# Two-layer decoder trunk: the filler matmuls at the three borders between sublayers are taken out

## What is computed

```python
def _layer(x, c, positions, w_ada, b_ada, g_pre_mix, g_post_mix, w_in, w_out,
           g_pre_ffn, g_post_ffn, w_gate, w_up, w_down):
    mod = jax.nn.silu(c) @ w_ada + b_ada
    sh1, sc1, gt1, sh2, sc2, gt2 = [m[:, None, :] for m in jnp.split(mod, N_MOD, axis=-1)]
    h = _rmsnorm(x, g_pre_mix) * (1.0 + sc1) + sh1
    proj = h @ w_in
    ...
    mixed = jax.nn.sigmoid(ga) * y_a + jax.nn.sigmoid(gb) * y_b
    x = x + gt1 * _rmsnorm(mixed @ w_out, g_post_mix)
    h = _rmsnorm(x, g_pre_ffn) * (1.0 + sc2) + sh2
    f = (jax.nn.silu(h @ w_gate) * (h @ w_up)) @ w_down
    return x + gt2 * _rmsnorm(f, g_post_ffn)
```

## Time and profile before

| | us |
|---|---|
| median of 3 runs | 896.37 (896.2 to 896.77) |
| the profiled execution, its own time | 897.06 |
| its span, first to last instruction | 895.3 |
| TensorE busy in the span | 873.5 (98%) |
| VectorE, ScalarE, GpSimd busy | 673.6, 415.1, 135.1 |

### The profile page before, as it was taken

The page is one execution under the profiler, slowest core; times in us unless marked ns, Lnnn a source line. Parts: engine busy times, 40 slices in busy tenths (PEclk is TensorE's granted clock), DMA queues, the critical chain, the costliest instruction groups (busy, mean ns, idle before and its releaser), DMA issues.

```text
span 895.3 us, 13320 instructions
## 1 busy us (share of the span) xinstructions
PE 873.5 (98%) x5121; PEld 757.1 (85%) x5121; DVE 673.6 (75%) x1090; ACT 415.1 (46%) x607; POOL 135.1 (15%) x164
## 2 busy tenths in 40 slices
PE   7999999999999999999999999999999999999996
PEld 5787788888878999999978778888887799999995
DVE  3778998888788787767768899988787855654842
ACT  1264644655545353354336455455564535434421
POOL 6500300200322030110232030020031100000302
PEclk9999999999999999999999999999999999999999
DMA  8788675666442968666634766666744274564511
GB/s 330 299 306 289 212 256 191 230 238 238 141 165 82 376 248 302 258 262 255 230 141 148 294 227 238 213 221 236 258 142 165 98 278 165 218 264 177 195 65 48
DMA packets 35584, 194.73 MB, mean 218 GB/s; under 512 B 4544, under 2 KB 4544, under 8 KB 19008
## 3 DMA queue, kind: packets, MB, share of 16 engines
q1 hardware_dynamic: 33984, 189.62, 57.4%
q0 software_dynamic: 1536, 4.24, 1.5%
HBM read 192.80 MB, written 1.05 MB: 217 GB/s over the span
## 4 chain that ended last, share of the span: by engine, by line
PE 82%; issue 8%; DVE 7%; POOL 1%; ACT 1%; DMA 0%; DVEq 0%; POOLq 0%; SPq 0%; ACTq 0%
PE ps L1150 24%; PE ps L1152 24%; PE ps L1151 24%; PE ps L1204 3%; PE ps L1304 2%; PE ps L1284 1%; PE ps L1256 1%; DVE pj L989 1%; DVE ffn_m L851 1%; DVE x L1012 1%; DVE pj L974 1%; PE ps L1277 1%; PE ps L1255 1%; PE ps L1276 1%; PE ps L1278 1%
## 5 line engine op out<-in xcount | busy, mean ns | idle before, releaser
L806 DVE TENSOR_TENSOR w_lo<-raw,w_hi 128x2048 fp32r<-128x2048 f32 (+1 forms) x132 | 302.2, 2299 | 49.8 <-ACT w_hi L580 48.0
L580 ACT ACTIVATE w_hi<-raw 128x2048 fp32r<-128x2048 f32 (+1 forms) x132 | 247.8, 1893 | 27.4 <-DMA raw<-w_stream 15.9
L1150 PE MATMUL ps<-w_hi,t_hi 128*128 128x512 f32 (+2 forms) x512 | 200.4, 391 | 2.3 <-DVE t_lo L954 1.5
L1152 PE MATMUL ps<-w_hi,t_lo 128*128 128x512 f32 (+2 forms) x512 | 194.1, 379 | 0.0
L1151 PE MATMUL ps<-w_lo,t_hi 128*128 128x512 f32 (+2 forms) x512 | 193.6, 378 | 0.0
L1150 PE MATMUL ps<-t_hi,w_hi 128*128 128x256 f32 x640 | 181.3, 283 | 0.0
L1152 PE MATMUL ps<-t_hi,w_lo 128*128 128x256 f32 x640 | 181.0, 283 | 0.0
L1151 PE MATMUL ps<-t_lo,w_hi 128*128 128x256 f32 x640 | 180.9, 283 | 0.0
L1151 PEld LDWEIGHTS ps<-t_lo,w_hi 128*128 128x128 f32 x640 | 122.6, 192 | 0.9
L1150 PEld LDWEIGHTS ps<-t_hi,w_hi 128*128 128x128 f32 x640 | 122.6, 192 | 0.8
L1152 PEld LDWEIGHTS ps<-t_hi,w_lo 128*128 128x128 f32 x640 | 122.6, 192 | 0.0
(11 more groups left out here) (178 smaller groups left out, 1045.5 us busy)
## 6 DMA issues: line engine op xcount, KB each, us to landing
raw<-w_stream SPq DMA_DIRECT2D x128, 1024.0 KB, 5.9
ada<-w_ada SPq DMA_DIRECT2D x84, 512.0 KB, 5.6
raw<-w_ada SPq DMA_DIRECT2D x6, 512.0 KB, 11.4
raw<-w_stream SPq DMA_DIRECT2D x4, 656.0 KB, 8.9
scale_t<-gains POOLq DMA_DIRECT2D x4, 512.0 KB, 4.0
gate_t<-gains POOLq DMA_DIRECT2D x4, 512.0 KB, 4.8
pj<-w_ada SPq DMA_DIRECT2D x3, 512.0 KB, 15.7
mixed<-w_ada SPq DMA_DIRECT2D x2, 512.0 KB, 12.1
```

Source lines behind the costliest of these rows:

```text
L580: nc.scalar.activation(w_hi[:, U % RING, 0:n], raw[:, U % RAW, 0:n], ACT.Copy).then_inc(s_hi, 1)
L806: nc.vector.tensor_tensor(w_lo[:, U % RING, 0:n], raw[:, U % RAW, 0:n], w_hi[:, U % RING, 0:n].bitcast(F32), ALU.subtract).then_inc(s_lo, 1)
L1150: nc.tensor.matmul(dst, hi, w_h, start=first, stop=False)
L1152: return nc.tensor.matmul(dst, lo, w_h, start=False, stop=last)
```

## The change

The two fills of each of the three borders are taken out: 16 + 4, 23 + 4 and 16 + 4 matmuls. The fillers of the start stay: the 14 behind the first `turn_h` are now under `if not l`. No wait, signal, buffer or other instruction is touched.

```diff
 START_FILL = (5, 5, 18, 11, 0, 8, 0, 4)
-MIXER_FILL, FFN_FILL, TURN_FILL = 16, 23, 4
 TURN_AT = 7
@@
             for l in range(DEPTH):
-                if l:
-                    fill(SCO, t_hi[:, 0, 0:P], t_hi[:, 0:2, :], 2 * SEQ, FFN_FILL)
                 turn_h(l, "h1", 0)
-                if l:
-                    fill(SCO, m_hi[:, 0, 0, 0:P], m_hi[:, 0, :, :], 2 * SEQ, TURN_FILL)
-                else:
+                if not l:
                     fill(2, ones[:, :], ones[:, :], P, 14)
                 project(l, 0, 0)
@@
                 out_unit(l, 3, 1)
-                fill(SCO, t_hi[:, 0, 0:P], t_hi[:, 0:2, :], 2 * SEQ, MIXER_FILL)
                 turn_h(l, "h2", 0)
-                fill(SCO, m_hi[:, 0, 0, 0:P], m_hi[:, 0, :, :], 2 * SEQ, TURN_FILL)
                 first_up(l, 0, lambda: turn_h(l, "h2", 1))
```

## The result

| | median us | runs | ratio to before |
|---|---|---|---|
| before | 896.57 | 896.20 to 896.77 | |
| changed | 901.67 | 900.43 to 902.25 | 1.0056 (95% interval 1.0042 to 1.0069) |

The change costs 5.1 us. (Here "before" has one run more than in the table ahead of the prediction, hence 896.57 for 896.37.) The profiled execution of the changed kernel took 902.25 us, its span is 900.5 us, 5.2 more than before. Forecast were 903.3 us, with a range of 897.8 to 905.8.

What follows compares the result with a forecast made beforehand. TensorE was taken to bound the kernel, with VectorE's chain ending the border waits. Fills as work saved 0; clock falls cost 2.45, 2.05 and 2.45 us, so 896.37 + 6.95 = 903.3 us, range 897.8 to 905.8.

Steps and rivals of the forecast that it cites:

- What bounds: Whole kernel: TensorE, busy for 873.5 us of a span of 895.3; VectorE's chain ends the border waits.
- part 1: Fills as work at the borders: removing them saves 0, bounded by 0 and 0.4 us.
- the forecast's: Clock falls at all three borders, 6.95 us in all, 903.3 us; chance 0.60.
- (a): At each border, transposes at the low level make `t_lo` 0.1 to 0.2 us late: +0.2 us.
- (b): Products behind each border run at half speed until the clock rises: 2.35 us lost (1.7 to 3.0).
- (c): TensorE's spare time ahead of the second transposes comes off: 0.1 us at first and third border, 0.5 at second.
- The second and third: Clock falls only at second border, 898.4 us, chance 0.16; or at two of three, 900.9 us, chance 0.11.
- The fourth: Clock stays up at all borders, fills did nothing: 896.4 us; chance 0.10.
- The fifth: Fills hold back VectorE, ScalarE or TensorE's queue during the border chain; at 10% without them 893.8 us; chance 0.03.

Runs made afterwards that it cites:

- experiment 2: Against the kernel before, the three times four fills behind the transposes out, the 55 long fills kept: 896.56 us, ratio 1.0004.
- experiment 5: Against the kernel before, long fills 8, 12, 8 for 16, 23, 16: 898.38 us, ratio 1.0017; with 24, 33, 24: 899.0 us, ratio 1.0026.
- experiment 4: Against the kernel before, each 512-column fill at the borders replaced by two 128-column transposes of the same tile: 896.26 us, ratio 0.9999.
- experiment 1: Against the kernel before, the 55 long fills out, the three times four behind the transposes kept: 899.42 us, ratio 1.0036.
- experiment 6: The changed kernel run once more, unaltered: 901.76 us, ratio 1.0056 to the kernel before.

## Why the prediction was right, and where its sum was off

**What bounds, and part 1 (fills cost nothing as work): right.** The transposes came 0.1 us sooner and the first product 0.1 us sooner by the profile; taken from the last real matmul (262.12 and 262.05) that is 0.03 us. Experiments 2 and 5 show the same from both sides.

**The case that came about is the forecast's:** falls at all three borders. The argument for it, that 6.6 us pass with only transposes in them, was not the right one. Transposes do count, by experiment 4, and four turn fills behind the idle time didn't prevent a fall, by experiment 1. The idle 4.2 us were enough alone, though I had taken the 4.9 us of the end as a sign that they might not be. The end shows a time after which the clock was down, not the shortest that brings it down; experiment 1 has falls after 3.0 and 2.0 us. In the five profiles with idle times of 4.2 us and more ahead of the transposes, all twelve such borders had a fall. So the case was the right one for a reason that was only in part right.

**The terms**, in us, by the starts of the first product, of the second transposes, and of the product that first follows these (in the changed kernel 470.60, 478.01 and 478.80 at the second border, 699.89, 707.54 and 709.55 at the third; before, 468.46, 474.23 and 475.30, and 696.43, 702.25 and 704.32):

| | first border | second | third | sum |
|---|---|---|---|---|
| (a), forecast | 0.2 | 0.2 | 0.2 | 0.6 |
| (a), measured: last matmul to first product | -0.03 | 0.06 | 0.02 | 0.05 |
| (b) less (c), forecast | 2.25 | 1.85 | 2.25 | 6.35 |
| (b) less (c), measured: first product to second transposes | 2.23 | 1.64 | 1.83 | 5.70 |
| second transposes to next product, forecast | 0 | 0 | 0 | 0 |
| the same, measured | -0.06 | -0.28 | -0.06 | -0.40 |

The measured terms make 5.35 us, as the spans do within 0.15 us; the forecast had 6.95. The 1.6 us between them are (a) with 0.55, (b) with 0.2, (c) with 0.45 and the third row with 0.4.

(a) was 0.2 at each border and is 0.06 at the most. The first four transposes were late as forecast: at the second border ScalarE's copy starts 1.15 us after them, where 0.69 us was usual at the first. But the copy ended at the moment at which VectorE got free:

```profile
468.56 1.21 DVE L995 TENSOR_TENSOR pj<-ps,gate_t 128x1024 f32<-128x1024 f32 x1
469.18 0.60 ACT L662 ACTIVATE t_hi<-ps 128x512 fp32r<-128x512 f32 x1 [2.89 <-PE ps L1203]
...
469.81 0.69 DVE L953 TENSOR_TENSOR t_lo<-ps,t_hi 128x512 fp32r<-128x512 f32 x1
```

VectorE is in the gate multiply of the other token tile until 469.77. So some 0.4 of the 0.46 us were hidden; I had worked out 0.1 to 0.2 us of lateness and taken the upper end.

(b) was sized well: 4.7 us at the low level after the first product were assumed (halfway between 3.4 and 6.0) and 5.3, 5.1 and 4.5 came. Not quite half of that is lost (0.23 against 0.43 us a product). That the middle was so close is in part luck. Neither way of counting from the start of the kernel fits (the clock was back 7.7, 7.7 and 6.9 us after the first transpose, not 6.0), and in the second profile of the same kernel the low level reached 3.2, 4.7 and 4.2 us into the products.

(c) was too small. I measured TensorE's spare time from the end of the last product, 0.39 us after its start; but the next instruction can start 0.23 us after it. So there were 0.26 us to spare at the first border and not 0.1, and 0.66 at the second and not 0.5 (a 256-column product there leaves the way free after 0.12 us). The third row of the table is of the same kind and was missing: the second group of four transposes waited for VectorE in the kernel before, so a TensorE that comes later finds both halves ready. At the second border this alone gives back 0.28 us.

That no wait further on takes up the loss held: the distance of 182.4 us behind the first border is unchanged, and so are those behind the second (214.04 against 214.10 us) and the third (182.39 against 182.40).

**The rivals.** The second and third (falls at one or two borders) are refuted for this kernel by its two profiles and by the mean clock of its other runs, and they describe better what happens with half the fills or without the turn fills. The fourth (the clock stays up) is refuted. The fifth (fills hold back the chain) is refuted by the first product, and by experiment 5.

## What to carry to other kernels

An engine that waits may have work that pays though nobody reads it. What a filler is worth is not in the wait that it fills but in the products behind it: here 67 free matmuls save three stretches of some 3 to 5 us of products at half the clock, less the 0.3 to 0.9 us that the engine had to spare. Size fillers so that they end just before the wait does (half of them weren't enough here; what lies between half and all wasn't tried), check the work behind them as well as the wait, and measure spare time of TensorE from when the next instruction could start, not from the end of the last.

## What the runs showed of the hardware

- Fillers behind a fall go at the low level themselves and can hold up real work: four of 512 columns took 2.05 us for 1.17, and the first product came 1.0 us later (experiment 1).
- The clock fell 2.0 us into an idle time (experiment 1, second border), and in the same code the moment of the fall moved from one execution to the next (experiment 6).
- What a low stretch costs depends on where it lies: one of 6.8 us that ended before the first product cost 0.05 us (experiment 1), one of the same length that reached 5.3 us into the products 2.15 us (the changed kernel, first border).
- A clock can fall although TensorE is never idle for over 1.1 us at a time: 0.57 us idle, 1.33 us of transposes and 1.07 us idle lay ahead of a fall at one border of three (experiment 2), and 3.23 us of idleness didn't at one border with half the fills (experiment 5).
- fp32 transposes alone keep the clock at 1.00 over the whole border, 6.8 us (experiment 4).
- With the clock in play the same program spreads more: 1.8 us between runs of the changed kernel and 2.4 with half the fills, against 0.6 to 1.3 for the kernel before and 0.5 with too many fills.
